# A decoder step in one kernel: the weighted one-hot rows of the PEER scatter, given to VectorE (three of four) and ScalarE (one of four)

## The reference, cut to what matters

```python
def chunk_fn(xc):
    ...
    cv, ci = lax.top_k(comb, PEER_TOPK)
    i1 = jnp.take_along_axis(si[:, :, 0], ci // PEER_TOPK, axis=-1)
    i2 = jnp.take_along_axis(si[:, :, 1], ci % PEER_TOPK, axis=-1)
    eidx = i1 * PEER_NKEYS + i2
    w = jax.nn.softmax(cv, axis=-1)
    u = u_tab[eidx]
    a = jax.nn.gelu(jnp.einsum('td,thkd->thk', xc, u, preferred_element_type=f32)) * w
    return jnp.einsum('thk,thkd->td', a.astype(v_tab.dtype), v_tab[eidx])
```

## Time and profile before

| | before |
|---|---|
| median of the runs shown | 3759.98 us |
| profiled execution: its time | 3762.34 us |
| its span, first to last instruction | 3760.5 us |
| mean granted TensorE clock over the span | 0.926 |
| TensorE busy (matrix products) | 3370.9 us, 90% |
| VectorE busy | 2484.4 us, 66% |
| ScalarE busy | 1668.4 us, 44% |
| GpSimd busy | 1219.8 us, 32% |
| first scatter stage | first instruction at 1784.32 us, last ends about 1876.7 us |
| second scatter stage | first instruction at 3023.05 us, last ends about 3116.2 us |

### The profile page before, as it was taken

The page is one execution under the profiler, slowest core; times in us unless marked ns, Lnnn a source line. Parts: engine busy times, 40 slices in busy tenths (PEclk is TensorE's granted clock), DMA queues, the critical chain, the costliest instruction groups (busy, mean ns, idle before and its releaser), DMA issues. The chain is left out here.

```text
span 3760.5 us, 64553 instructions
## 1 busy us (share of the span) xinstructions
PE 3370.9 (90%) x20784; PEld 2955.4 (79%) x20784; DVE 2484.4 (66%) x4739; ACT 1668.4 (44%) x3326; POOL 1219.8 (32%) x1084
## 2 busy tenths in 40 slices
PE   7988799999369998798799999997889889999997
PEld 7963589898359886697688999987669877899996
DVE  7979678786958644578944555564366985455555
ACT  4430344545044442354744444454245474444443
POOL 1526212120612100047963333310002976433332
PEclk9985799999589998899999999998589999999999
DMA  5520278785038652344055555544014404555554
GB/s 184 186 99 0 86 257 331 253 325 186 0 116 317 218 177 84 124 162 145 0 184 173 184 184 186 183 169 147 23 67 147 148 25 151 173 184 184 187 183 149
DMA packets 163122, 590.78 MB, mean 157 GB/s; under 512 B 18596, under 2 KB 19364, under 8 KB 162728
## 3 DMA queue, kind: packets, MB, share of 16 engines
q1 hardware_dynamic: 143824, 521.92, 41.2%
q10 hardware_dynamic: 19160, 67.18, 4.7%
HBM read 587.96 MB, written 1.06 MB: 157 GB/s over the span
## 5 line engine op out<-in xcount | busy, mean ns | idle before, releaser
L314 PEld LDWEIGHTS ps<-hT,parts 128*128 128x128 f32 x12864 | 1596.3, 193 | 105.0 <-POOL parts L138 34.2
L314 PE MATMUL ps<-hT,parts 128*128 128x256 f32 x12864 | 1614.3, 285 | 68.5 <-POOL parts L138 30.2
L138 DVE TENSOR_TENSOR parts<-ring,parts 128x512 fp32r<-128x512 f32 x1786 | 1187.5, 700 | 571.9 <-ACT parts L133 562.6
L133 ACT ACTIVATE parts<-ring 128x512 fp32r<-128x512 f32 x1930 | 1157.1, 628 | 601.1 <-PE ps L314 567.7
L314 PE MATMUL ps<-parts,gatedT 128*128 128x512 f32 x4128 | 1011.4, 397 | 8.0 <-DVE parts L138 7.9
L314 PEld LDWEIGHTS ps<-parts,gatedT 128*128 128x128 f32 x4128 | 762.6, 189 | 175.0 <-POOL gatedT L1044 8.3
L1180 POOL TENSOR_TENSOR gatedT<-acted,iota 128x256 fp32r<-128x256 f32 x264 | 195.0, 739 | 1399.2 <-PE ps L314 1165.7
L138 POOL TENSOR_TENSOR parts<-ring,parts 128x512 fp32r<-128x512 f32 x144 | 223.1, 1572 | 585.3 <-ACT parts L133 585.0
L1151 ACT ACTIVATE acted<-ps 128x256 f32<-128x256 f32 x264 | 101.1, 383 | 591.5 <-PE ps L314 591.5
L1183 POOL TENSOR_TENSOR gatedT<-acted,gatedT 128x256 fp32r<-128x256 f32 x264 | 311.4, 1180 | 20.8
L1164 DVE TENSOR_TENSOR acted<-acted,big 128x256 f32<-128x256 f32 x176 | 74.9, 425 | 357.8 <-ACT acted L1151 357.8
(11 more groups left out here) (295 smaller groups left out, 2363.9 us busy)
## 6 DMA issues: line engine op xcount, KB each, us to landing
ring<-wts SPq DMA_DIRECT2D x965, 512.0 KB, 3.4
big<-mod_wts ACTq DMA_DIRECT2D x112, 512.0 KB, 4.8
big<-rows SPq DMA_DIRECT2D x15, 512.0 KB, 5.2
big<-mod_bias ACTq DMA_DIRECT2D x14, 512.0 KB, 4.2
big<-mod_rows SPq DMA_DIRECT2D x4, 512.0 KB, 4.4
big<-peer_keys SPq DMA_DIRECT2D x2, 1024.0 KB, 5.2
x<-x_in SPq DMA_DIRECT2D x1, 1024.0 KB, 5.0
big<-s_bc ACTq DMA_DIRECT2D x4, 256.0 KB, 3.3
```

The source lines that it names most:

```text
L133: act.activation(self.part(n, half, 0), self.raw(n, half), ACT.Copy).then_inc(self.hi_done, 1)
L138: v.tensor_tensor(self.part(n, half, 1), self.raw(n, half), self.part(n, half, 0).bitcast(F32), ALU.subtract).then_inc(self.lo_done, 1)
L314: last = pe.matmul(out, a(x), b(y), start=start and x + y == 0, stop=stop and x == 1)
```

## The change

The third of each four tokens' `one2` row goes from GpSimd to VectorE, which so makes tokens 0, 1 and 2. GpSimd's block in the stage, its semaphore and TensorE's wait for it are taken out.

```diff
@@ -58,7 +58,7 @@
-ON_VECTOR, ON_GPSIMD, ON_SCALAR = (0, 1), (2,), (3,)
+ON_VECTOR, ON_SCALAR = (0, 1, 2), (3,)
@@ -1856,7 +1856,7 @@
-    with stage(k, "first second_v second_p second_a far scattered act_stored weighted") as (s, block):
+    with stage(k, "first second_v second_a far scattered act_stored weighted") as (s, block):
@@ -1891,23 +1891,11 @@
-        @block.gpsimd
-        def _(pool):
-            def group(g, j, i):
-                b = j % 2
-                if not known(g) or g >= 2:
-                    pool.wait_ge(s["scattered"], g - 1)
-                second(pool, g, b, ON_GPSIMD).then_inc(s["second_p"], 1)
-
-            for g in range(groups):
-                group(g, g % 4, 0)
-
         @block.tensor
         def _(pe):
             def group(g, j, i):
                 b = j % 2
                 pe.wait_ge(s["second_v"], g + 1)
-                pe.wait_ge(s["second_p"], g + 1)
                 pe.wait_ge(s["second_a"], g + 1)
```

## The result

The changed kernel takes 3787.47 us (median of 4 runs, 3783.48 to 3789.24) beside 3760.95 us for the kernel before (4 runs): ratio 1.0065, 95% interval 1.0052 to 1.0078. It is slower by 26.5 us by the medians, 24.4 by the ratio (the interval allows 20 to 29). The forecast of 3785.0 lies 2.5 us off.

What follows compares the result with a forecast made beforehand. VectorE's issue rate was taken to bound the scatter: 2 x 60 x 0.204 = 24.5 plus 2 x 0.256 = 0.5, together 25.0 us on a median of 3759.98, gave 3785.0 us; 8-in-10 range 3774 to 3801.

Steps and rivals of the forecast that it cites:

- The pace: In the scatter stages VectorE's issue rate sets the period; a third `one2` makes it 1.604 us against 1.400.
- 0.06 in every other group: Between VectorE's `one2` in the scatter: 0.32 us falls to 0.26 once GpSimd's operation is gone.
- 0.05 at `one1`: VectorE's last step before the next `one1`, waiting for TensorE in every other group: 0.28 us, taken as 0.23 always.
- the slow distance: A 0.32 us start-to-start step behind a `one2` in every other scatter group, put down to GpSimd's phase.
- Three limits at 1.40: In the scatter, VectorE's issue rate and VectorE's and GpSimd's loops through TensorE all give 1.40 us a group.
- the two-buffer loop: Scatter makers start group g + 2 only after TensorE ends group g; VectorE's loop grows to 1.48 us, below 1.604.
- Groups 0 to 3 and the ends: Scatter stage's first groups run at TensorE's pace, no added time; each stage's end adds 0.256 us, 0.5 together.
- 1 (GpSimd holds VectorE up): In the scatter, removing GpSimd speeds VectorE more than the added row slows it: -18 us, 3742 us; chance 0.03.
- 2 (register work between the `one2`): In the scatter loop, register work causes the 0.32 us distance, which stays: 39 us more, 3799 us; chance 0.15.
- 3 (the clock): TensorE's clock falls in the scatter, a group taking about 1.73 us: 40 us more, 3800 us; chance 0.05.
- Rival 4: In the scatter, GpSimd's loop was the pace, not VectorE; priced within the case of time staying at 3760, chance 0.04.

Runs made afterwards that it cites:

- e1: Kernel before with token 2's `one2` row left out, so GpSimd idle and VectorE still making two rows; 4.7 us less than before, one run.
- e4: Kernel before with VectorE making all four `one2` rows, GpSimd and ScalarE none; 53.7 us more than before, one run.
- e5: Kernel before with four buffers for `one1` and `one2` in place of two, rows divided as before; 9.2 us less than before, one run.
- g4: Changed kernel with four buffers for `one1` and `one2` in place of two; 17.7 us more than the kernel before, one run.
- e2: Changed kernel with GpSimd also making token 2's row into a spare buffer nobody reads; 28.1 us more than the kernel before, one run.
- e8: Kernel before, two buffers, with one of each 16 rows moved from VectorE to ScalarE (7, 4 GpSimd, 5); 12.7 us more than before, one run.
- e7: Kernel before with four buffers and one of each 16 rows moved from VectorE to ScalarE (7, 4 GpSimd, 5); 6.0 us less than before, one run.
- g2: Four buffers, rows 7 VectorE, 4 GpSimd, 5 ScalarE of each 16, timed in turn with the kernel before; ratio 0.9966 (0.9954 to 0.9978).
- g3: Kernel before with four buffers, rows divided as before, timed in turn with the kernel before; ratio 0.9978 (0.9969 to 0.9987).

## Why the prediction was right

*The pace.* The step that VectorE's issue rate sets the period held within 0.003 us: 1.604 forecast, 1.601 measured. So did its price, 0.256 from start to start. The duration would have misled: 0.385 us is the mean of a `one2` before, and 0.385 x 120 would have given 46 us. That the median of the times came within 2.5 us of the forecast is in part luck: the same two kernels lie 26.5 us apart in one comparison and 19.8 in the other, and the profiled execution spent 3.1 us less outside the stages.

*What the removal gives back.* I took off 0.06 in every other group and 0.05 at `one1`, 0.05 us a group, and the changed kernel has neither (1.345 + 0.256 = 1.601). The reason that I gave for the 0.06, a fixed phase to GpSimd's operation, holds: without GpSimd the slow distance is gone in e1, e4 and the changed kernel, and with GpSimd at another phase it is all but gone in e5. The work of GpSimd alone does not make it.

*Three limits at 1.40.* VectorE's rate alone would be 1.345, as e1 (nearly) and e5 show. What made 1.40 of it was the two-buffer loop together with the phase of GpSimd's operation. Naming the loop mattered little for this change, since at three rows it has some 0.24 us to spare in two groups, and g4 shows no gain from deeper buffers in the period. For the kernel before it is what was worth mending.

*Groups 0 to 3 and the ends* I counted at 0 and 0.5 us. From first `one1` to group 4 the stages take 0.6 us more and 0.0 more, so the zero holds. With 59 periods, not 60, between groups 4 and 63 the sum is 2 x 59 x 0.201 = 23.7, and 24.3 with the first groups; behind the last `one1` comes the third `one2`, twice 0.3 us up to the end of the last products. From the first `one1` to those the two stages take 24.9 us more, where I had summed up 25.0.

*The rivals.* 1 (GpSimd holds VectorE up) fell by e1 and e2, 2 (register work between the `one2`) by the changed kernel, e1 and e4, 3 (the clock) by the clock of 1.00 in every middle stretch, at a TensorE share of 72% and of 62%. Rival 4 asked whether VectorE was the pace at all. It was, but with 0.05 us on top from the coupling through TensorE. In weighing rival 1 I read 1.33 us of GpSimd inside a period of 1.40 as speaking against exclusion. That was too quick, as the last section shows: part of that 1.33 is waiting.

## What to carry to other kernels

When work moves to an engine that is full from start to start, price it by the distance between starts of back-to-back instructions, not by the duration, and check that distance at two counts of the instruction. An engine that is slow at an operation still helps if its time is hidden: GpSimd took five times VectorE's 0.256 us for a row, part of it waiting, and carried it for 0.05 us of VectorE's time. Where several limits meet at one number, deepen the buffers first: it takes the loops away, and then rows can be moved from the fullest engine to whoever has time, but not in the other order (e8). And when two engines both look full, ask whose starts follow its own rate, and which of the makers ended last before the consumer began (e7, e8).

## What the runs showed of the hardware that was not expected

GpSimd, not VectorE, pays where the two meet. The same 128x128 operation took a median of 1.331 us in the kernel before and 0.90 in e2, and in e8, where VectorE had a gap, it took 0.79 (timelines of GpSimd and VectorE in e8, then in e7, where L1890 is `one1` as well):

```profile
1829.78 0.79 POOL L1881 TENSOR_SCALAR tmp<-iota,pickT 128x128 f32<-128x128 f32 x1
```

```profile
1830.31 0.69 DVE L1890 TENSOR_TENSOR tmp<-iota,pickT 128x512 f32<-128x512 f32 x1 [0.28 <-issue]
```

```profile
1829.22 0.69 DVE L1890 TENSOR_TENSOR parts<-iota,pickT 128x512 fp32r<-128x512 f32 x1
1831.92 0.68 DVE L1890 TENSOR_TENSOR parts<-iota,pickT 128x512 fp32r<-128x512 f32 x1
```

```profile
1829.52 1.16 POOL L1881 TENSOR_SCALAR tmp<-iota,pickT 128x128 f32<-128x128 f32 x1
1832.00 1.36 POOL L1881 TENSOR_SCALAR tmp<-iota,pickT 128x128 f32<-128x128 f32 x1
```

In e8 it starts 0.53 us ahead of `one1`, beside the multiplication, which reads one operand from PSUM, and takes 0.79, the last 0.26 of it beside `one1`. In the kernel before it starts together with `one1`, whose 512 columns come from two operands in SBUF, and takes 0.54 us longer. In e7 it starts 0.30 us after `one1` and takes 1.16, or 0.08 after it and takes 1.36. The end is what stays: 1.46 and 1.44 us after the start of `one1`, about the 0.69 of `one1` and the 0.79 of an undisturbed operation. All 466 operations of GpSimd that start 0.07 to 0.4 us after a `one1` in e5, e7, g2 and g3 end 1.43 to 1.47 us after its start, as if each were held until `one1` is over. This fits the Trainium skill (SBUF — State Buffer, "Who interferes with whom"), by which a VectorE operation with two SBUF inputs shuts out a GpSimd operation that reads SBUF, and one with a PSUM input and a single SBUF input does not. Its "fully blocks" holds in these rows for GpSimd; VectorE in turn lost 0.06 us to it at most in one distance of the middle stretches (0.09 once, at the start of e5's loop), also where GpSimd's operation was the first to start by its row (1829.92 and 1829.97). No kernel changed `one1` alone, so that it is the cause rests on these positions.

VectorE's recorded durations grow through the stage in the changed kernel, for `one1` from 0.69 us in group 4 to 0.79 in group 63, while the distances from start to start stay at 1.601. Nothing waits for it by these rows. It is one more reason to read starts.
